# Router on the raw tokens with modulated weights, in a one-core diffusion step with a mixture of experts

## The reference, cut to what matters

```python
h = rmsnorm(x, norm2[i]) * (1.0 + sc2) + sh2     # sc2, sh2: one pair for latent, one for context tokens
s = jax.nn.sigmoid((h @ w_router).astype(F32))   # (tokens, 16)
sb = s + router_bias                             # choose a group of 4 experts, then the best 2 in it
...
gate = sum(one_hot(eid) * w)                     # w: the two s, divided by their sum
act = silu(h @ w_gate) * (h @ w_up) * gate       # every expert, its own tokens
return act @ w_down
```

## Time and profile before

| what | value |
|---|---|
| three runs | 1852.25, 1856.09, 1856.32 us (median 1856.09) |
| profiled execution: its time / its span | 1850.06 / 1848.3 us |
| PE busy | 1733.5 us, 94% |
| DVE / ACT / POOL busy | 642.8 / 251.3 / 180.8 us |
| granted clock of PE, mean | 0.982 |

### The profile page before, as it was taken

How to read it: one execution, slowest core, us unless ns; L and a number is a source line. 1 busy time by engine, 2 the same in 40 slices (tenths; PEclk the granted TensorE clock), 3 DMA queues, 4 the chain that set the end, 5 groups by cost and what they waited for, 6 DMA issues and landing times.

```text
span 1848.3 us, 17397 instructions
## 1 busy us (share of the span) xinstructions
PE 1733.5 (94%) x6466; PEld 976.4 (53%) x6466; DVE 642.8 (35%) x1111; ACT 251.3 (14%) x538; POOL 180.8 (10%) x274
## 2 busy tenths in 40 slices
PE   5999999999999999999989999898999999899995
PEld 2764374644755456644456444354666664554442
DVE  2333322434233333333363323322333324433324
ACT  5000000000000000000121111321323221111111
POOL 1000000000000100011001222110000000012221
PEclk9999999999999999999999999999999999999998
DMA  9423452124412152122485999830000023659994
GB/s 339 163 91 137 144 216 91 46 91 137 148 45 90 55 187 87 45 91 91 116 289 166 342 342 346 260 121 0 23 16 11 7 64 136 224 162 343 344 339 138
DMA packets 159360, 281.24 MB, mean 152 GB/s; under 512 B 11428, under 2 KB 106424, under 8 KB 154184
## 3 DMA queue, kind: packets, MB, share of 16 engines
q1 hardware_dynamic: 144616, 236.39, 36.7%
q0 software_dynamic: 9248, 33.61, 7.0%
q10 hardware_dynamic: 5440, 10.49, 1.6%
HBM read 247.09 MB, written 33.37 MB: 152 GB/s over the span
## 4 chain that ended last, share of the span: by engine, by line
PE 78%; SPq 8%; DMA 6%; DVE 4%; ACT 2%; issue 2%; ACTq 0%; POOL 0%; DVEq 0%; POOLq 0%
PE banks L1127 15%; PE banks L1017 10%; PE banks L992 8%; PE banks L1201 6%; PE banks L1322 4%; SPq L601 4%; PE banks L1421 4%; SPq L602 3%; PE banks L1111 3%; PE banks L1119 3%; PE banks L1218 3%; PE banks L1102 2%; PE banks L891 2%; PE banks L1354 2%; PE banks L1353 2%
## 5 line engine op out<-in xcount | busy, mean ns | idle before, releaser
L1127 PE MATMUL banks<-wr 128*128 128x512 f32 x640 | 281.3, 592 | 0.0
L1201 PE MATMUL banks<-wr,arena 128*128 128x512 f32 x512 | 226.3, 595 | 10.0 <-DMA wr<-in_moe_w_down 7.0
L1127 PEld LDWEIGHTS banks<-wr 128*128 128x128 f32 x640 | 119.4, 190 | 139.7 <-issue 139.7
L1017 PE MATMUL banks<-wr 128*128 128x256 f32 x768 | 173.1, 385 | 4.0 <-ACT arena L1533 2.3
L1017 PEld LDWEIGHTS banks<-wr 128*128 128x128 f32 x768 | 147.7, 193 | 29.0 <-issue 4.5
L1201 PEld LDWEIGHTS banks<-wr,arena 128*128 128x128 f32 x512 | 94.7, 190 | 120.5 <-issue 119.8
L992 PE MATMUL banks<-wr,arena 128*128 128x512 f32 x320 | 143.3, 603 | 3.2 <-ACT arena L1527 3.2
L1218 PE MATMUL banks<-wr,arena 128*128 128x512 f32 x256 | 115.4, 593 | 0.9 <-ACT arena L1621 0.9
L992 PEld LDWEIGHTS banks<-wr,arena 128*128 128x128 f32 x320 | 60.5, 193 | 74.3 <-issue 72.2
L1567 ACT ACTIVATE arena<-banks 128x512 f32<-128x512 f32 x40 | 23.9, 597 | 520.4 <-PE banks L1127 520.4
L816 POOL DMA_INDIRECT acc_dram<-arena,put_ids x30 | 60.5, 2016 | 264.6 <-DVE arena L2078 264.6
(11 more groups left out here) (271 smaller groups left out, 2020.7 us busy)
## 6 DMA issues: line engine op xcount, KB each, us to landing
wr<-in_w_ada SPq DMA_DIRECT2D x24, 2048.0 KB, 7.6
wr<-in_moe_w_gate SPq DMA_DIRECT2D x32, 1024.0 KB, 13.5
wr<-in_moe_w_up SPq DMA_DIRECT2D x32, 1024.0 KB, 16.0
wr<-in_moe_w_down SPq DMA_DIRECT2D x32, 1024.0 KB, 15.6
wr<-in_ret_w_in SPq DMA_DIRECT2D x12, 2048.0 KB, 10.6
wr<-in_ret_w_in SPq DMA_DIRECT2D x8, 1024.0 KB, 8.6
wr<-in_ret_w_out SPq DMA_DIRECT2D x4, 2048.0 KB, 7.9
arena<-mod_rows_dram SPq DMA_DIRECT2D x14, 512.0 KB, 6.4
```

What stands on the lines that cost most here:

```text
L1017: mm = mmul(dst[:, r * 256:r * 256 + 256], lhs, rhs, start=(start and r == 0 and k == 0), stop=(k == 3), skip_group_check=True)
L1127: mm = mmul(bank[i % 3][:], hT[:, k, tile_cols(t)], ring8(2 + r)[:, k, :], start=(k == 0), stop=(k == KT - 1))
L1201: mm = mmul(bank[2][:], xgT[:, e.par, k, :], expert_w(e.buf)[0][:, k].rearrange("p g f -> p (g f)"), start=(k == 0), stop=(k == KT - 1))
```

## The change

The router no longer waits for h2. With h = x · rs · scale + shift, h @ W is rs · (x @ (scale · W)) + shift @ W. DVE makes the modulated weights (`w_mod`, for latent and for context) and the shift's products (`w_shift`) once per layer (`router_weights`). PE transposes raw x; one more product with `ones` sums the shift part. DVE multiplies the sums by `rs` and adds the shift (`logits`). Tile 4's transposes go to two banks of their own and wait for x only; the 8 idle products ahead of them are gone. ACT takes one sigmoid of a spare column at tile 2, so that the table is there early. The row h2 of tile 4, which only the experts need now, is made by ACT (x times `rs`) and POOL (times the scale row, plus the shift row) behind the sigmoid. The ten products of the token numbers take `sent` as weights in four column groups; ACT copies the partial sums and one more product adds the groups. `rows_T(1)` moves behind the router.

```diff
             def moe(l):
                 n = 2 * l + 1
                 rstd(n)
+                pool.wait_ge(S("used"), (n + 1) * NT)
+                pool.wait_ge(S("rows_in"), 96 * l + 96)
+                ch.link(g.tensor_tensor(h2b[:, 0, :], h2b[:, 0, :], rows[:, 0, 1, :], ALU.mult))
+                g.tensor_tensor(h2b[:, 0, :], h2b[:, 0, :], rows[:, 1, 1, :], ALU.add).then_inc(S("h2_ready"), 1)
                 pool.wait_ge(S("h2_first"), 16 * l + 16)
...
             def h2_T(l, t):
-                pe.wait_ge(S("h2_ready"), l * NT + t + 1)
-                if t:
+                if l == 0:
+                    pe.wait_ge(S("x_add"), 10 * RH - 10 + 2 * t + 2)
+                else:
+                    pe.wait_ge(S("mx_add"), 2 * t + 2)
+                last = t == NT - 1
+                if t and not last:
...
-                    mm = tpose(banks(0, 2)[:, tile_cols(k)], h2b[:, t % 4, tile_cols(k)], ident[:])
+                    mm = tpose(banks(RAW_BANK[l] if last else 0, 2)[:, tile_cols(k)], x[:, t, tile_cols(k)], ident[:])
...
+                    pe.wait_ge(S("rt_w"), l + 1)
+                    mmul(bank[R_BANK[l]][:, P:P + 2 * NE], ones[:], w_shift, start=True, stop=True)
...
             def moe(l):
+                h2_T(l, NT - 1)
                 router(l, NT - 2)
-                if l == 0:
-                    pe.wait_ge(S("op_evac"), 10 * RH)
-                idle_products(IDLE_BANK[l], 8)
-                h2_T(l, NT - 1)
                 router(l, NT - 1)
                 router_sum(l, NT - 1)
+                if l == 0:
+                    rows_T(1)
+                    pe.wait_ge(S("op_evac"), 10 * RH)
+                else:
+                    pe.wait_ge(S("mo_evac"), 10)
                 idle_products(IDLE_BANK[l], 20)
...
                 for q in range(2 * NT):
-                    mm = mmul(bank[6][:, 0:32], onehot[:, q, :], sent[:, q].rearrange("p o e -> p (o e)"),
-                              start=(q == 0), stop=(q == 2 * NT - 1))
-                mm.then_inc(S("ids_mm"), 1)
+                    g = q % 4
+                    mm = mmul(bank[6][32 * g:32 * g + 32, P:2 * P], sent[:, q].rearrange("p o e -> p (o e)"), onehot[:, q, :],
+                              start=(q < 4), stop=(q + 4 >= 2 * NT), tile_position=(0, 32 * g))
+                mm.then_inc(S("rt_sum"), 1)
+                pe.wait_ge(S("rt_copied"), (l + 1) * (NT + 1))
+                mmul(bank[6][:, 0:32], sums_T, pick32[:], start=True, stop=True).then_inc(S("ids_mm"), 1)
...
             for t in range(NT):
-                square(1, t)
                 if t:
                     h2_evac(0, t - 1)
+                square(1, t)
+                if t == 2:
+                    A_(spare[:], half[:], ACT.Sigmoid)
...
             def moe(l):
+                h2_evac(l, NT - 1)
                 router_copy(l, NT - 2)
-                h2_evac(l, NT - 1)
                 router_copy(l, NT - 1)
-                act.wait_ge(S("rt_sum"), l * NT + NT)
-                A_(rt[0].rearrange("p t e -> p (t e)"), bank[R_BANK[l]][:, 0:NT * NE], ACT.Sigmoid).then_inc(S("sig_s"), 1)
+                act.wait_ge(S("logits"), l + 1)
+                A_(rt[0].rearrange("p t e -> p (t e)"), rt[1].rearrange("p t e -> p (t e)"), ACT.Sigmoid).then_inc(S("sig_s"), 1)
+                act.wait_ge(S("rstd"), (2 * l + 2) * NT)
+                act.wait_ge(S("h2_first"), 16 * l + 16)
+                A_(h2b[:, 0, :], x[:, PT, :], ACT.Copy, scale=rs[:, PT:PT + 1]).then_inc(S("used"), 1)
+                if l == 0:
+                    rows_evac(1)
+                act.wait_ge(S("rt_sum"), (l + 1) * (NT + 1))
+                A_(sums_T, bank[6][:, P:2 * P], ACT.Copy).then_inc(S("rt_copied"), 1)
...
+            def router_weights(l):
+                dve.wait_ge(S("modB"), l + 1)
+                dve.wait_ge(S("misc_in"), 48)
+                e8 = lambda ap: ap.rearrange("p (k e) -> p k e", k=KT)
+                wide = lambda j, c: mod[:, l, 8 * j:8 * j + 8, c].unsqueeze(2).to_broadcast([P, KT, NE])
+                for c in range(2):
+                    ch.link(v.tensor_tensor(e8(w_mod[:, c * P:c * P + P]), e8(w_rt[:, 0:P]), wide(4, c), ALU.mult))
+                    ch.link(v.tensor_tensor(e8(w_tmp), e8(w_rt[:, 0:P]), wide(3, c), ALU.mult))
+                    ch.link(v.tensor_reduce(w_shift[:, c * NE:c * NE + NE], w_tmp.rearrange("p (k e) -> p e k", k=KT), AX.X, ALU.add))
+                v.memset(w_mod[:, 2 * P:2 * P + NE], 0.0).then_inc(S("rt_w"), 1)
+
+            def logits(l):
+                bank_r = bank[R_BANK[l]]
+                dve.wait_ge(S("rt_sum"), l * (NT + 1) + NT - 1)
...
+                dve.wait_ge(S("rt_sum"), l * (NT + 1) + NT)
+                v.scalar_tensor_tensor(out=rt[1][:, PT, :], in0=bank[ST_BANK[l]][:, P:P + NE], scalar=rs[:, PT:PT + 1],
+                                       in1=w_tmp[:, NE:2 * NE], op0=ALU.mult, op1=ALU.add).then_inc(S("logits"), 1)
...
             mod_rest(1, 48)
+            router_weights(0)
             op_evac(RH)
...
             dve.wait_ge(S("g1_in1"), 32)
+            router_weights(1)
...
-                h2_rows(1, t)
+                if t < NT - 1:
+                    h2_rows(1, t)
             moe(1)
```

More of the change, by code:

```diff
@@ L66 @@
 COPIES = {"p1": 1, "PR": 2, "C11": 3}
+RAW_BANK = (4, 2)
 T_BANK = {0: (4, 6, 0, 2, 4), 2: (0, 0, 0, 0, 0)}
@@ L180, in build @@
         stage = sb("stage", [P, 512])
-        pick16 = sb("pick16", [P, NE])
-        pick2 = pick16[:, 0:2]
+        pick32 = sb("pick32", [P, 2 * NE])
+        pick16, pick2 = pick32[:, 0:NE], pick32[:, 0:2]
+        spare = sb("spare", [P, 1])
         w_rt = sb("w_rt", [P, KT * NE + NE])
@@ L304, in build @@
         onehot = M["xgT"][:, 0:10 * P].rearrange("p (q n) -> p q n", n=P)
+        sums_T = M["xgT"][:, 10 * P:11 * P]
+        w_mod = M["rt"][:, 640:912]
+        w_shift = M["rt"][:, 912:944]
+        w_tmp = M["rt"][:, 944:1072]
         pairs = M["rt"][:, 640:760].rearrange("p (q e) -> p q e", e=6)
@@ L948, in router_sum @@
             def router_sum(l, t):
-                pe.wait_ge(S("rt_copied"), l * NT + t + 1)
-                mmul(bank[R_BANK[l]][:, t * NE:(t + 1) * NE], s_T[:, tile_cols(t)], pick16[:], start=True, stop=True)\
+                pe.wait_ge(S("rt_copied"), l * (NT + 1) + t + 1)
+                dst = bank[ST_BANK[l]][:, P:P + NE] if t == PT else bank[R_BANK[l]][:, t * NE:(t + 1) * NE]
+                mmul(dst, s_T[:, tile_cols(t)], pick16, start=True, stop=True)\
                     .then_inc(S("rt_sum"), 1)
@@ L1509, in h2_evac @@
                     act.wait_ge(S("router_mm"), l * NT + t - 1)
-                A_(h2T[:, t % 2, 0:4, :].rearrange("p k n -> p (k n)"), bank[0], ACT.Copy).then_inc(S("hTa"), 1)
+                A_(h2T[:, t % 2, 0:4, :].rearrange("p k n -> p (k n)"), bank[RAW_BANK[l] if t == NT - 1 else 0], ACT.Copy)\
+                    .then_inc(S("hTa"), 1)
             def router_copy(l, t):
@@ L1732, in _ @@
             for t in range(NT):
-                square(3, t)
                 if t:
                     h2_evac(1, t - 1)
+                square(3, t)
+                if t == 2:
+                    A_(spare[:], half[:], ACT.Sigmoid)
                 if t >= 2:
@@ L1787, in h2_rows @@
             def h2_rows(l, t):
-                n, c = 2 * l + 1, 1 if t == PT else 0
+                n, c = 2 * l + 1, 0
                 if t == 0:
@@ L1806, in h2_evac @@
                     dve.wait_ge(S("router_mm"), l * NT + t - 1)
-                v.tensor_copy(h2T[:, t % 2, 4:8, :].rearrange("p k n -> p (k n)"), bank[1]).then_inc(S("hTd"), 1)
+                v.tensor_copy(h2T[:, t % 2, 4:8, :].rearrange("p k n -> p (k n)"), bank[RAW_BANK[l] + 1 if t == NT - 1 else 1])\
+                    .then_inc(S("hTd"), 1)
+            def router_weights(l):
[11 more added lines that the diff above has]
+                dve.wait_ge(S("rt_sum"), l * (NT + 1) + NT - 1)
+                dve.wait_ge(S("rstd"), (2 * l + 1) * NT + NT)
+                ch.link(v.tensor_copy(w_tmp[:, 0:2 * NE], bank_r[:, P:P + 2 * NE]))
+                four = rt[1][:, 0:PT, :]
+                ch.link(v.tensor_tensor(four, bank_r[:, 0:PT * NE].rearrange("p (t e) -> p t e", t=PT),
+                                        rs[:, 0:PT].unsqueeze(2).to_broadcast([P, PT, NE]), ALU.mult))
+                ch.link(v.tensor_tensor(four, four, w_tmp[:, 0:NE].unsqueeze(1).to_broadcast([P, PT, NE]), ALU.add))
+                dve.wait_ge(S("rt_sum"), l * (NT + 1) + NT)
+                v.scalar_tensor_tensor(out=rt[1][:, PT, :], in0=bank[ST_BANK[l]][:, P:P + NE], scalar=rs[:, PT:PT + 1],
+                                       in1=w_tmp[:, NE:2 * NE], op0=ALU.mult, op1=ALU.add).then_inc(S("logits"), 1)
             dve.wait_ge(S("gset"), 20)
@@ L1838, in op_evac @@
                             h2_evac(0, t - 1)
-                        h2_rows(0, t)
+                        if t < NT - 1:
+                            h2_rows(0, t)
```

20 lines of the change are left out of this document (8 added, 12 removed).

## The result

The changed kernel takes 1858.84 us (median of 9 runs, 1854.2 to 1863.09), the kernel before 1852.62 (9 runs): 1.004 times as long, 95% interval 1.0027 to 1.0053, that is 5 to 10 us more. I had forecast 1857.2 and "no change". The time lies in the range, but part of that is luck: I had set out from a median of 1856.09, and the kernel before turned out 3.5 us faster over more runs. What I had forecast is a difference of +1.15 us; the medians differ by 6.2. It is a small slowdown where I had expected none.

What follows compares the result with a forecast made beforehand. The chain of waits, three quarters PE, was taken as the bound, with engines waiting for one another around both routers. Terms of +1.1 us (layer 0) and +0.05 (layer 1) gave 1857.2 us from a median of 1856.09; range 1847.5 to 1862.

Steps and rivals of the forecast that it cites:

- Router's stretch: Last addition to x to the sigmoid's end: 5.3 to 6.2 us instead of 10.98, gain taken as 5.3 per layer.
- Token numbers: Ten router-shaped products instead of ten full ones: 1.6 us against 2.43, gain taken as 0.6, ends 0.2 and 0.8.
- DVE held by POOL: Choice of experts: POOL's two operations on tile 4's row make DVE's two-operand instructions wait, 4.3 us lost per layer.
- the mirror image of one row: POOL's `rstd` instruction took 1.17 instead of 0.19 us under DVE instructions; DVE was assumed to wait for POOL likewise.
- POOL lets DVE pass: Choice of experts: DVE runs through in 14 us beside POOL; named as what would above all make the prediction wrong.
- the first two rivals: DVE not held by POOL: with the gather slowed 1848.6 us, chance 0.16; with neither 1845.4, chance 0.06.
- The gather among loads: Each layer's first gather falls into the later weight loads: 2.5 us more, ends 0 and 5.5.
- served behind the loads: Slower rival at each layer's first gather: price 5.5 instead of 2.5 us, total 1863.2, chance 0.09.
- the shift product: One added PE product per layer between the projection's products: 0.40 us, partly under its neighbours, cost taken as 0.2.
- the router weights: DVE's `router_weights`, 2.05 us: nothing lost in layer 0, layer 1's first copy and PE's projection 0.75 us late.
- Sum: Adds the terms: +1.1 us in layer 0, +0.05 in layer 1, together +1.15, no change.

Runs made afterwards that it cites:

- the kernel with too many idle products: Changed kernel with 60 instead of 20 idle products before the choice of experts and 68 instead of 30 before the first transposes: 1867.37 us, ratio 1.0079.
- loads first: Changed kernel with SyncE issuing the next experts' weight loads ahead of the write of h2's tile 4: 1848.42 us, 0.9979 of the kernel before.
- four-operation kernel: Changed kernel with four POOL operations on tile 4's rows instead of two (shift added, taken off, added again): 1864.45 us, one run.
- late loads: Kernel before with one wait added, so that weight loads are issued only when the choice of experts is in: 1861.57 us, ratio 1.0045.
- the kernel with the later router weights: Changed kernel with layer 1's modulated router weights made behind DVE's first two copies instead of ahead of them: 1859.22 us, 1.0033 of the kernel before.
- Fitted idle products: Changed kernel with 42 instead of 20 idle products before the ranks and 40 instead of 30 before the first gathered transposes: 1852.00 us, ratio 0.9996.
- the kernel before with fewer idle products: Kernel before with 15 instead of 30 idle products ahead of the first gathered transposes: 1851.43 us, ratio 0.9989.
- the rows by DVE: Changed kernel with tile 4's normed rows made by DVE again, ACT's copy and POOL's two operations gone: 1851.60 us, 1.0002 of the kernel before.

## Why the prediction was right or wrong

**Router's stretch: right.** 5.30 us in both layers, against 5.3 to 6.2: a gain of 5.7, my upper end.

**Token numbers: right at one speed only.** From the one-hot tile to the numbers it took 2.51 us before. With TensorE at full speed it is 1.72 and 1.73 (the kernel with too many idle products), a gain of 0.8, my upper end. In the changed kernel it is 2.32 and 1.89: the eight idle products between the ranks and the token numbers ran at 1.2 GHz and in layer 0 ended 0.65 us after the one-hot tile was ready. With loads first it is 3.05 and 2.93, as the token products themselves were slow too (1.50 us in layer 0 instead of 0.85), and the shorter form loses 0.5. I had bounded that case at a gain of 0.2.

**DVE held by POOL: the mechanism right, the price a little high.** I took 4.3 from the mirror image of one row; two stretches of 1.95 and 2.00 in place of 0.18 make 3.6. The four-operation kernel gives 1.95 for each. "POOL lets DVE pass" is out, and with it the first two rivals.

**The gather among loads: right, a little low.** I took +2.5; it is +3.3 and +3.1. It isn't served behind the loads (that would be +5.5). Loads first and late loads show both directions.

**Sum of the steps as far as the transposes: right, in part by luck.** From the end of the last addition to the first transposes, layer 0 went from 32.19 to 33.21 us, +1.02, where I had +1.1 (+0.9 without the 0.2 of the shift product, which falls ahead of the last addition). The four terms were each off by 0.4 to 0.8 us and cancelled: the router gave 0.4 more than forecast and the hold cost 0.7 less, the token numbers gave 0.4 less and the gather cost 0.8 more. Layer 1 fell by 1.5, where I had +0.05 (-0.9 without the 0.2 and the 0.75 of the router weights, which fall outside too and measured 0.70).

**The sum's missing term.** The step that failed is "Sum". It ends at the first transposes and takes for granted that whatever comes later is moved as it is. I had used TensorE's lower speed only as a bound for two small groups of products, though the later gather that I had forecast was bound to keep TensorE waiting. It is a term: the first expert's products behind that wait, and the products around the token numbers, in part at 1.2 GHz. From the transposes to the second expert the profiled execution took 1.42 and 1.65 us more than the kernel before, and the kernel with the later router weights, whose code is the same there, 3.81 and 2.71 more. Fitted idle products, which change nothing else, take back 6.8 us, as much as the whole loss of 6.2 by the medians. With them the changed kernel stands at 0.9996 of the kernel before, -3.5 to +2.0 us; my +1.15 for the other terms lies in that.

**What stays open.** The gap between the 6.8 and 7.1 us that fitted idle products are worth by the medians and the kernel before with fewer idle products, where the same slow clock cost nothing in the median. The two stretches of the profiled executions give 2.7 us from the changed to the fitted kernel, 7.5 from the one with the later router weights to the fitted one, and 3.4 with the rows by DVE; single traces don't settle the medians' figure.

## What to carry to other kernels

When a wait ahead of TensorE gets longer, price the products behind the wait too: read the granted clock from the end of the wait to the next full stretch, and fit the idle products to the new wait by their measured time. When a row is moved to POOL, look at what DVE does at that moment: here each POOL operation of 128x1024 (2.36 us) held up one small DVE instruction with two SBUF operands until it ended. When a write that opens a queue of loads is made later, look at what runs into those loads; here the order of write and loads in SP's queue was worth more than the change itself.

## What was not expected of the hardware

TensorE in the kernel before with fewer idle products idled 1.94 us ahead of its layer 1 transposes, and its granted clock to the second expert was 0.87. The Trainium skill, page "TensorE: Matmul & The Clock Gate", section "Part 1: The HAM clock gate", calls the throttled clock the default state, which activity releases; the rows agree: the clock was 0.57 from 1631 to 1634 us, 0.86 to 1637 and 1.00 to 1640. Of the 28 stretches in the table's clock column, 14 had an idle time of 1.9 to 3.6 us ahead, and their clock is 0.70 to 0.87; the other 14 had at most 1.04, and it is 1.00.

The same wait doesn't always hit the same products. Ahead of the ranks TensorE waits 2.82 or 2.83 us in the kernel before and its two variants. In five of these six stretches the ranks still ran at full speed (0.45, 1.00 and 0.43 us) and the clock fell in the eight idle products behind them (0.58 from 972.17 to 975.39 in layer 0 of the kernel before), which cost nothing where it rose again before the token numbers. In layer 0 of the one with late loads the ranks themselves ran at 1.2 GHz (0.72, 1.81 and 0.69 us).

A first gather of the same size landed in 4.3 to 6.3 us where the issue of the last load had ended at least 3.4 us before it (12 stretches), and in 8.0 to 9.4 us where it had ended at most 3.2 us before or was still going on (16 stretches).
